# Attention with split V as the stationary operand, turned probabilities split and moving in half sequences, and part of the preparation on GpSimd

## What is computed

```python
q = rmsnorm(q, q_head_norm); k = rmsnorm(k, k_head_norm)   # 16 heads of 96 = 64 + 32
q = apply_rope(q, pos); k = apply_rope(k, pos)
s = einsum('bqhd,bkhd->bhqk', q, k) / sqrt(96)
p = softmax(s, axis=-1)
o = einsum('bhqk,bkhd->bqhd', p, v)                        # v: 64 wide
return o.reshape(b, L, 1024) @ w_out
```

## Time and profile before

| | |
|---|---|
| time, median of 3 runs | 3041.29 us (3038.35 to 3042.91) |
| span of the profiled execution | 3038.7 us |
| attention heads, first to last score reduction | 121.88 to 634.79 us |
| PE busy over the span | 2967.0 us (98%) |
| DVE, ACT, POOL busy over the span | 1924.1, 1176.6, 1527.5 us |

### The profile page before, as it was taken

One profiled execution on the slowest core, in us unless ns is written; L12 is line 12 of the kernel. 1 busy time (PEld: TensorE's weight loads), 2 busy tenths in 40 slices (PEclk: granted clock), 3 DMA queues, 4 the chain that ended last, 5 costly groups with the idle time before them and its releaser, 6 DMA issues.

```text
span 3038.7 us, 50018 instructions
## 1 busy us (share of the span) xinstructions
PE 2967.0 (98%) x19166; PEld 2684.5 (88%) x19166; DVE 1924.1 (63%) x2960; ACT 1176.6 (39%) x2027; POOL 1527.5 (50%) x997
## 2 busy tenths in 40 slices
PE   8999999999999999999999999999999999999998
PEld 8999999999999999999999988677777788888776
DVE  6677777755534445777788851677778934445666
ACT  4465666641333334553111122232323533334552
POOL 4100000043777777765444444467674577777774
PEclk9999999999999999999999999999999999999998
DMA  3000100021223334442233423333333232235442
GB/s 128 26 30 27 37 26 16 16 100 49 72 95 99 103 100 163 140 144 71 87 117 94 138 90 118 116 119 101 123 94 118 67 107 102 99 103 171 149 130 90
DMA packets 195934, 286.73 MB, mean 94 GB/s; under 512 B 14709, under 2 KB 105077, under 8 KB 195701
## 3 DMA queue, kind: packets, MB, share of 16 engines
q1 hardware_dynamic: 156096, 236.23, 23.8%
q10 hardware_dynamic: 39605, 47.34, 4.7%
HBM read 208.64 MB, written 74.86 MB: 93 GB/s over the span
## 4 chain that ended last, share of the span: by engine, by line
PE 80%; DVE 7%; POOL 5%; issue 4%; DMA 2%; ACT 1%; SPq 1%; DVEq 0%; ACTq 0%; POOLq 0%
PE PS L1272 72%; PE PS L1528 4%; PE PS L1513 2%; DMA Wraw<-in_w 1%; POOL Wlo L1108 1%; POOL Wlo L1168 1%; PE PS L1872 1%; POOL SQ L1213 1%; SPq L911 0%; DVE GD L3627 0%; POOL RMS L1178 0%; POOL Wraw L1126 0%; POOL Wraw L1124 0%; DVE MX L3007 0%; PE PS L2024 0%
## 5 line engine op out<-in xcount | busy, mean ns | idle before, releaser
L1272 PE MATMUL PS<-Uhi,Whi 128*128 128x352 f32 (+2 forms) x2028 | 512.4, 328 | 16.5 <-DVE Ulo L2799 13.8
L1272 PE MATMUL PS<-Uhi,Wlo 128*128 128x352 f32 (+2 forms) x2028 | 507.3, 326 | 0.0
L1272 PE MATMUL PS<-Ulo,Whi 128*128 128x352 f32 (+2 forms) x2028 | 507.0, 326 | 0.0
L1108 POOL TENSOR_TENSOR Wlo<-Wraw,Whi 128x512 fp32r<-128x512 f32 x242 | 329.8, 1366 | 130.4 <-ACT Whi L2442 127.1
L1272 PEld LDWEIGHTS PS<-Uhi,Whi 128*128 128x128 f32 x2028 | 340.9, 189 | 39.4 <-issue 15.9
L1067 POOL TENSOR_TENSOR Whi<-Wraw,const 128x1024 fp32r<-128x1024 f32 x64 | 159.1, 2486 | 418.4 <-PE PS L1272 403.4
L1272 PEld LDWEIGHTS PS<-Ulo,Whi 128*128 128x128 f32 x2028 | 343.5, 189 | 20.3
L1272 PEld LDWEIGHTS PS<-Uhi,Wlo 128*128 128x128 f32 x2028 | 343.4, 189 | 19.5
L2442 ACT ACTIVATE Whi<-Wraw 128x512 fp32r<-128x512 f32 x242 | 151.3, 629 | 330.7 <-POOL Wraw L1126 133.3
L1156 POOL TENSOR_TENSOR Olo<-H,Ohi 128x1056 fp32r<-128x1056 f32 x5 | 12.1, 2444 | 521.8 <-ACT Ohi L2345 521.8
L1272 PE MATMUL PS<-T,Whi 128*128 128x264 f32 (+1 forms) x1328 | 219.1, 288 | 2.1 <-DVE H L3311 1.9
(11 more groups left out here) (431 smaller groups left out, 7114.4 us busy)
## 6 DMA issues: line engine op xcount, KB each, us to landing
Wraw<-in_w SPq DMA_DIRECT2D x192, 256.0 KB, 3.0
Wraw<-in_w SPq DMA_DIRECT2D x91, 512.0 KB, 3.7
Wraw<-in_w SPq DMA_DIRECT2D x168, 128.0 KB, 2.7
xt<-XTT ACTq DMA_DIRECT2D x20, 640.0 KB, 5.7
opd<-HID SPq DMA_DIRECT2D x40, 264.0 KB, 3.4
T<-opd SPq DMA_DIRECT2D x18, 528.0 KB, 4.3
Ulo<-opd SPq DMA_DIRECT2D x17, 528.0 KB, 4.8
Ulo<-opd SPq DMA_DIRECT2D x17, 512.0 KB, 5.5
```

Of the source, the lines that this page charges most:

```text
L1108: pool.tensor_tensor(f.oplo[j % SLOTS], FIRST_S2 if (p, k) == (0, 6) else f.factors[k], f.ophi[j % SLOTS].bitcast(F32), ALU.subtract).then ...
L1272: ins = pe.matmul(out, lhsT, rhs, start=start, stop=stop, skip_group_check=True)
```

## The change

- The product with V takes split operands, and its sides are exchanged. `VH[x % 2]` holds, for each key block, 128 columns: 64 of V's high part in the head's own half and 64 of its low part in the other half. It is stationary. The turned probabilities are split too (`PTH` by ACT in `high_turned`, `PTL` by DVE in `low_turned`) and are collected over a sequence, so that half a sequence (264 queries) is the moving operand: `outputs(x, s, h)` is ten matmuls of 264 columns, four times a head, in the steps 4, 6, 9 and 11 after the head's first (`PV_TURNS`; 11 is n = 1 of the next head). One half of the result partitions is then copied by ACT (`other_half`) and added to the other by DVE (`add_outputs`), one step later, right into `H`. The result is already turned, so `turn_outputs` and `take_outputs_of` go.
- 1 / sum is applied to the finished pair: `invert` once a pair, `turn_sums`, `take_sums`, `save_sums`, `load_sums` (through memory, as with the key factors) and a multiply of 128 x 1056 (`scale_outputs`). The last pair is spread by PE (`spread_sums`) and scaled by DVE (`scale_last`).
- POOL takes over `turn_queries`, `low_q`, `scale_keys`, `low_k`, `low_weights` from DVE, and gets `low_values` and `scale_outputs`. All key high parts (`high_k`) stay on ACT, and so does the new `high_values`.
- The maximum's first result goes to PSUM instead of SBUF. The squares of keys go to `SQ`; queries and scaled keys have two buffers; V has one. The last head's scores alternate between two pairs of banks throughout. Semaphores reused later are counted on from their new totals.

```diff
         def turn_probs(t):
             pe.wait_ge(p_full, t + 1)
-            if t:
-                pe.wait_ge(pt_vector, t)
-                pe.wait_ge(pt_scalar, t)
             for b in range(KB):
+                if t and b in (0, TURN_FIRST):
+                    pe.wait_ge(pt_low, 2 * t - (b == 0))
...
-        def outputs(t):
...
-            for b in range(KB):
-                ins = pe.matmul(PS[0:CW, A_OUT, 0:VD], PT[t % 2][:, b, :],
-                                V[x // 4 % 2][:, n // KB * KB + b, x // 2 % 2, x % 2 * VD:(x % 2 + 1) * VD],
...
+        def outputs(x, s, h):
+            pe.wait_ge(pt_high, 2 * last_block(x, s, h) + 2)
+            pe.wait_ge(pt_low, 2 * last_block(x, s, h) + 2)
+            pe.wait_ge(v_lo, x + 1)
+            if (x, s, h) != (0, 0, 0):
+                pe.wait_ge(o_evicted, half_number(x, s, h))
+            of = slice(h * QHALF, (h + 1) * QHALF)
             for b in range(KB):
+                low = PTL[b // TURN_FIRST][:, b % TURN_FIRST, of]
+                for i, probs in enumerate((PTH[:, b, of], low)):
+                    ins = mm(PS[:, A_OUT, 0:QHALF], VH[x % 2][:, s * KB + b, :], probs,
+                             start=(b == 0 and i == 0), stop=(b == KB - 1 and i == 1))
             ins.then_inc(ov_full, 1)
...
# ACT, in each step
                 if t >= 1:
-                    take_turned(t - 1)
-                if t >= 0:
-                    exponentials_of(t)
-                if t >= 2:
-                    evict(t - 2)
+                    high_turned(t - 1)
+                exponentials_of(t)
+                if half_at_turn(t, 1):
+                    other_half(*half_at_turn(t, 1))
+                if j and j % 4 == 0 and n == 1:
+                    high_values(j)
                 if nxt < HEADS:
-                    if n == 5:
+                    if n == 3 and nxt % 4:
+                        high_values(nxt)
+                    if n == 6:
                         high_q(nxt)
-                    if n == (1 if nxt % 2 else 6):
+                    if n == (7 if nxt % 2 == 0 else 2):
                         high_k(nxt)
...
+        def high_turned(t):
...
+            for b, (k0, k1) in enumerate(((0, TURN_FIRST), (TURN_FIRST, KB))):
+                act.wait_ge(pt_full, 2 * t + b + 1)
...
+                act.activation(PTH[:, k0:k1, key_start(n) + dup:key_start(n) + CW], ... ACT.Copy)
...
# DVE, in each step
                 if t >= 1:
-                    take_turned(t - 1)
-                    invert(t - 1)
+                    low_turned(t - 1)
+                if half_at_turn(t, 1):
+                    add_outputs(*half_at_turn(t, 1))
+                if j and j % 2 == 0 and n == 1:
+                    invert(j // 2 - 1)
                 if nxt < HEADS:
                     if nxt % 2 == 0 and n < 2:
                         key_factors(nxt // 2, n)
-                    if n == (0 if nxt % 2 else 5):
-                        scale_keys(nxt)
-                    if n == 4:
-                        turn_queries(nxt)
-                    if n == (7 if nxt % 2 else 6):
-                        low_q(nxt)
-                    if n == (2 if nxt % 2 else 7):
-                        low_k(nxt)
-                    if n in ((6, 9) if nxt % 2 else (8, 9)):
+                    if n in (8, 9):
                         query_factors(nxt, n == 9)
-                if j >= 0 and split_unit(j) is not None and n == (2 if j % 2 else 5):
-                    low_weights(j)
...
+            most = PS[0:CW, score_bank(t), QHALF:QHALF + 1]
+            step(vec.tensor_reduce(most, PS[0:CW, score_bank(t):score_bank(t) + 2, 0:QHALF], AX_XY, ALU.max))
...
# POOL, in this order for each head
+            if nxt % 2:
+                scale_keys(nxt)
+            if j and j % 4 == 0:
+                low_values(j)
+            if nxt % 2:
+                low_k(nxt)
+            if nxt % 4:
+                low_values(nxt)
+            if j % 2 and split_unit(j) is not None:
+                low_weights(j)
+            if j >= 4 and j % 2 == 0:
+                scale_outputs(j // 2 - 2)
+            turn_queries(nxt)
+            if j % 2 == 0 and split_unit(j) is not None:
+                low_weights(j)
+            if nxt % 2 == 0:
+                scale_keys(nxt)
+            low_q(nxt)
+            if nxt % 2 == 0:
+                low_k(nxt)
```

More of the change, by code:

```diff
@@ L397, in prep_orders @@
             stats.append(("k", (nxt + 1) // 2))
-    prep += [("o", PAIRS - 1, s) for s in range(NSEQ)]
     return {n: i for i, n in enumerate(prep)}, {n: i for i, n in enumerate(stats)}
@@ L869, in _ @@
         for p in range(1, PAIRS):
+            if p >= 2:
+                save_sums(p - 2)
+                load_sums(p - 2)
             if p % 2:
@@ L1009, in load_feed @@
             load_factors_down(f)
+        save_sums(PAIRS - 2)
+        load_sums(PAIRS - 2)
         sp.wait_ge(qs_ready, HEADS)
@@ new lines, in _ @@
+        low_q(0)
+        pool.wait_ge(k_hi, 1)
+        low_k(0)
+        low_values(0)
+        for j in range(HEADS):
+            nxt = j + 1
+            if nxt == HEADS:
+                scale_outputs(PAIRS - 2)
+                break
+            if nxt % 2:
[18 more added lines that the diff above has]
+                low_k(nxt)
@@ L2355, in _ @@
         high_k(0)
+        high_values(0)
         for j in range(HEADS):
@@ L2385, in _ @@
         t = HEADS * PER_HEAD
-        take_turned(t - 1)
-        evict(t - 2)
-        evict(t - 1)
-        take_outputs_of(PAIRS - 1, 1)
+        high_turned(t - 1)
+        for h in range(2):
+            other_half(HEADS - 1, 1, h)
         high_out(PAIRS - 1)
@@ L3046, in _ @@
         take_factors(0)
-        turn_queries(0)
+        turn_first_queries()
         scale_first_keys(0, 4)
         scale_first_keys(1, 0)
-        low_q(0)
-        low_k(0)
         query_factors(0, 0)
```

380 lines of the change are left out of this document (223 added, 157 removed).

## The result

The changed kernel takes **3110.39 us** (median of 4 runs, 3106.53 to 3111.89) beside 3040.72 us for the kernel before on the same chip: ratio 1.0226, 95% interval 1.0211 to 1.0240. It is 70 us slower. The forecast was 3050 with a range from 3029 to 3074: the sign was right, the size was not.

What follows compares the result with a forecast made beforehand. Bounds: PE's work and a 2.95 us chain per step. Head classes (+7.3, -0.6, -2.3, +4.7) and small terms made +9 us on the 3038.7 us span, 3048; the median lies 2.6 above, so 3050, range 3029 to 3074.

Steps and rivals of the forecast that it cites:

- The chain of 2.95 us: Plain attention steps: reduction, multiply, exponentials and next scores in series take 2.95 us, whatever PE work is saved.
- PE's blocks: Output blocks of ten matmuls make PE's steps uneven: n = 1 3.38 us, n = 4 3.33, with V n = 9 5.3.
- DVE in n = 0: Before even heads add_outputs waits for ACT's copy, then key_factors follows: 4.05 us, 1.1 over the chain.
- the first rival: PE's relief comes through: n = 0, 2, 8 at the chain, weights in time; 17 us less, 3033; chance 0.20.
- The weights: Heads 4, 8, 12, n = 6: POOL's low_weights comes late and PE waits 1.0 us (0.5 to 2.5).
- n = 6 before a key: The step with an output block and 12 projection matmuls of a key was put at 3.87 us.
- The maximum in PSUM: Writing the maximum's first result to PSUM in all 160 steps was taken to cost nothing (-5 to +8 us).
- query_factors in n = 8 and 9: DVE's query factor chain placed in these steps was said to make them 3.33 and 3.1 us.
- The clock: PE's clock expected to hold; rival: it falls in one or two steps a head, +10 to +20 us, chance 0.10.
- POOL holds DVE: Rival: DVE's factor chains in the heads meet POOL instructions, 20 to 40 us, 3070 to 3080 in all; chance 0.17.
- Start and ends: Start +0.6 us from POOL holding DVE's query factors; head 14 -0.8, last head +0.3; end nothing.
- The second and third rival: POOL holding DVE's factor chains (3070 to 3080, chance 0.17) and PE's clock falling in light steps (3060 to 3070, 0.10).

Runs made afterwards that it cites:

- e11_best: e7_combo with fillers also in the last two heads and output gap, query projection 14 + 4 matmuls, take_k behind the maximum: 3042.15 us, ratio 0.9999.
- e2_fill: The changed kernel plus 16 unread matmuls filling PE's wait in step 8 of the seven heads before a key: 3094.53 us, ratio 1.0168.
- e10_balance: e7_combo with fillers at the ends too, output blocks in steps 5 and 7, query sums in step 4, projection 14 and 4 matmuls: 3106.14 us.
- e3_psum: The changed kernel with the intermediates v and tmp of even heads' factor chains in PSUM, no operation reading SBUF twice: 3099.85 us, ratio 1.0194.
- e5_order: The changed kernel with key_factors ahead of add_outputs in step 0 and scale_outputs behind low_q, so low_weights comes earlier: 3107.20 us, ratio 1.0211.
- e8_nofill: e7_combo without its fillers, only the known waits taken away: 3075.52 us, ratio 1.0107.
- e4_before_qf8: The kernel before with one line changed, query_factors of odd heads in steps 8 and 9 instead of 6 and 9: 3073.04 us, ratio 1.0095.
- e7_combo: The changed kernel with query_factors in step 6, even heads' chains as in e3_psum, both moves of e5_order, fillers in steps 5, 7, 8: 3049.73 us.

## Why the prediction was wrong, step by step

- **The chain of 2.95 us**: right. Plain steps are 2.93 to 2.98 us. The saving of PE under the chain is lost, as said: PE waits 49.9 us for the exponentials ahead of scores, 12.2 before.
- **PE's blocks**: right. n = 1 3.40 (said 3.38), n = 4 3.36 (3.33), n = 9 before V 4.39 (5.3, too much). n = 2 behind `high_weights` 3.46 (3.45), but in two heads of four only.
- **DVE in n = 0**: right, 4.16 for 4.05, and 3.39 when the order was changed. But the first rival, which gave 1.1 us a head for it, left out that n = 1 then rises by 0.46.
- **The weights**: right. 5.63 against 4.60 us, the 1.0 said, in three heads, and gone with the earlier split. That POOL takes 2.4 us an operation was taken from the earlier trace rows and holds (2.42 to 2.46).
- **n = 6 before a key**: 3.87 said, 4.60 measured, 5 us in all. The lateness of `take_k`, 0.8 us, falls between the reductions of n = 6 and n = 7 as well as between n = 7 and 8; it was counted once. The kernel before had shown it, with 4.39 us in this step for 3.6 of PE's work, and with `take_k` behind the maximum (e11_best) the step took 3.96. In heads 2 and 10 the clock made it 5.4.
- **The maximum in PSUM**: right, the reduction takes 714 ns, 707 before, and the plain step is unchanged.
- **query_factors in n = 8 and 9: the step that failed.** It was costed on DVE alone (3.33 and 3.1 us between two reductions), less than `take_k` and PE's block, which set these steps at 3.46 and 3.33 us. That its first operation is also what frees the bank in which PE adds the key's squares in n = 8 was not followed. Measured: 69.7 us for n = 8 and 9 of the seven heads where 47.5 were said, +22 us. Of these the wait itself is 2.6 us (e2_fill, 50.1 us with the wait in and the clock held) and the clock behind it the rest. The kernel before with this line alone lost 31 us, 27 of them by the clock.
- **The clock: the term at nothing that failed with it.** The sum expected it to hold; as a rival it had the right kind, but was sized too small, at 10 to 20 us and 0.10. The argument was that a plain step's 11 matmuls in 2.95 us are more than the 29 records in 5 us of the earlier trace rows at which it held. That reading was wrong: 11 in 2.95 us are 3.7 a microsecond, 29 in 5 us are 5.8, so the new step did less than the row that held, and the row, from another stage, gave no ground for 1.00. In the changed kernel the granted clock was 0.90. It fell beside tiny sums, behind pauses of 2.25, 1.49, 0.98 and 0.67 us; but pauses of 1.49, 0.98 and 0.66 us in the same places also left it at 1.00, so the length of the pause alone does not decide. Its price was 27 us in the one pair of runs (against 4 for the waits there) and 26 in the other. I had priced one or two steps of scores at half clock; it stayed down for one to four steps, with all that PE does in them.
- **POOL holds DVE: a rival, right in mechanism, too large in total (20 to 40 us) and wrong in its place.** I had 0.65 us in n = 8 of four heads. It was 1.1 and 1.5 us in one chain in the picture above, and in the heads before V, where I had nothing, 0.6, 1.6 and 0.3 us (0.81, 1.75 and 0.51 us for 0.17 in head 7): n = 8 of the seven heads before an even one 39.8 us for 25.9, +14 us. POOL's own operations were not lengthened by DVE (2.44 us on average, as in the earlier trace rows). The forecast's timing had POOL idle during a chain of 1.4 us; but a chain needs to be clear of *every* POOL instruction, and a late wait shifts the one against the other. The Trainium skill, "SBUF — State Buffer", section "Who interferes with whom", says that a DVE instruction with at most one SBUF input outside the two-port modes does not contend, and one with two does. The traces agree: 1.69 (changed kernel), 2.32 and 2.33 us (e10_balance) for two-input operations under POOL, 0.17 and 0.18 for such work with one input in PSUM (e3_psum). One input in SBUF was not enough to be free of it: the 1.23 and 0.81 us are `tensor_scalar` operations with one.
- **Start and ends**: at the start two operations of the query's factors took 0.81 and 2.37 us for 0.17, as said in kind, but the first reduction came 1.0 us earlier, not 0.6 later. The last two heads took 2.5 us more, where -0.5 was said. Behind the heads 0 was said and 4.6 us measured. As the rest varies by 12 us between kernels with the same code there, this is open.

So the forecast counted the work nearly right: with the waits, the lock and the clock taken away, the steps of the changed kernel are within 0.7 us a head of what was expected of them. That its median is then 3049.7 us, the number forecast, is partly luck: two terms of the forecast (7 us by the expectation of e5_order) are out of that kernel too, and 212 matmuls are in it. What failed are one dependency that was not followed and a clock put at nothing. The second and third rival had single chances, where they came together: waits brought the clock down, and so did the light steps without them (e8_nofill). The Trainium skill, "TensorE: Matmul & The Clock Gate", section "A second HAM failure mode: psum-queue depth-cycling", warned that short idle spells between groups of matmuls make the clock swing. The traces agree, in that pauses of 0.67 to 2.25 us did so at many places, though not at every one, and give the price here; I had put it below a count of records.

## What to carry to other kernels

When a step is moved within an in-order engine, list the buffers that its first operation frees, not only what its last one makes ready, and go through every engine that wants them. A pause of PE of a microsecond can cost several: price it also at what follows at half clock (between 1.4 and some 6 us in a head where the clock fell, nothing where it held), and if the work can't be spread, fill the pause with matmuls that nobody reads (8 in each of seven heads brought back 27 us). Tiny chains on DVE beside a busy POOL should keep their intermediates in PSUM: at most one operand from SBUF in two-input operations, and none in `tensor_scalar`, as in e3_psum.

## What had not been expected of the hardware

- The clock fell behind a pause of 0.98 us in e4_before_qf8, a kernel that but for one line is the one with PE busy 98% of the span, and stayed at 0.50 for some 13 us although PE was busy all the time by its records (40 of 67 were transposes, sums of two columns and matmuls of 64 columns). The same pause in two other heads of the same execution did nothing.
- One DVE operation on 106 x 10 elements can last as long as a whole POOL instruction (2.32 and 2.33 us beside 2.44 and 2.41), and two such in a row take turns with two POOL instructions.
- Outside the heads the same code took between 2524.8 and 2537.5 us in the profiled executions of fourteen kernels. Ten executions of one of them, e7_combo, differ by 15 us. What decides this was not tried.
